# Expert layer of a decoder step: two of three prompt tiles by dense streamed tables instead of gathered rows

## The chip, the cores and the metric

One core of one Trainium2 chip runs the whole kernel. The metric is the device time of one launch in microseconds, median of several runs. The core has TensorE (PE; its weight loads are shown as PEld), VectorE (DVE), ScalarE (ACT), GpSimd (POOL) and SyncE (SP), and 16 DMA engines that move data between device memory and SBUF for all of them. SP and ACT start plain transfers; POOL starts the gathers that take row numbers from SBUF.

## The reference

One layer of a decoder on 512 prompt tokens and 32 sample tokens (8 sequences of 4), model width 1024, all in f32. A mixing part (projection, chunked gMLP, dilated window attention, output projection) comes first and is not touched. Then the expert layer (PEER), with 128 x 128 = 16384 experts, each a row of 1024 in `u_tab` and one in `v_tab`:

```python
q = (xb @ w_q).reshape(T, 8, 2, 128)
s = einsum('thcd,hcnd->thcn', q, sub_keys)      # 128 scores for each half key
s1, i1 = top_k(s[:, :, 0], 16); s2, i2 = top_k(s[:, :, 1], 16)
cand = s1[..., :, None] + s2[..., None, :]      # 16 x 16 pairs
top_s, pos = top_k(cand, 16); eid = (i1 * 128 + i2) at pos
g = softmax(top_s)
hid = gelu(einsum('thkd,td->thk', u_tab[eid], xb))
y = einsum('thk,thkd->td', g * hid, v_tab[eid]) # 8 heads x 16 = 128 experts a token
```

The layer's result is added to x, and a last RMSNorm gives y.

## The kernel before

Tokens lie in five tiles: tiles 0 to 3 of 128 prompt tokens and tile 4 (`SAMP`) with the 32 samples. `uv_tab` holds the u and the v row of an expert side by side, 8 KB. A slot is one of the 128 (head, rank) places of a token: one gather by POOL fetches for a slot one row for each of the 128 tokens of a tile. For the samples four groups of 32 partitions take four slots at a time, so 32 gathers do.

Tile 0 runs ahead, beside projection and attention of the others: 128 gathers of u rows (4 KB each, `gather_u`) are dotted with x on VectorE (`dots_to`, L1694). After attention 128 gathers of v rows (`gather_v`), now one token's 128 experts per gather, are weighed on TensorE (`weigh`, L896, four tokens at once in four column groups) into `acc`. These weighings are spread over the instruction stream of TensorE by `weigh_first(n)`: in `project_out` (output projection of tiles 1 to 4, L798), after `turn_xn` and in `half_queries` (L851). `JOBS` are the query projections, one for each head over tiles 1 to 4 (416 tokens); three of the eight run before the gathers of tile 1 start, the other five are put between the slots of tile 1 (`job_part`). `key_scores` (L871) multiplies by the sub keys.

Then for tiles 1, 2, 3 and the samples, 416 slots in one long loop, with a ring of `XR` = 6 buffers of 8 KB per partition:

- POOL: `gather_both` fetches u and v rows of a slot when the buffer is free.
- VectorE: `dot` (L1703) multiplies the u rows with x and sums, one hidden value per token. Between the dots run the 12 `LINKS` of each head's `route` (two rounds of top 8 of each half, candidates, top 16, one-hot pick of the numbers, L1547 to L1609), each link a step that waits for the one before.
- ScalarE: `weigh_slot` takes gelu of the hidden value (L1253), times the gate, and writes a diagonal matrix of the weights (`diag`, L1003).
- TensorE: `add_slot` (L907) multiplies diagonal and v rows, 2 x 512 columns, and sums in PSUM (`acc`).
- 20 slots of tile 1 (`BY_DVE`) are added by VectorE instead (`add_rows`, L1711).

After each tile ScalarE reads the sum (`read_sum`), squares it, and VectorE scales it (`finish_y`, L1724); SP stores y. Each engine runs its instructions in the order in which they are written; semaphores tie them.

## Time and profile before

| | |
|---|---|
| median of 3 runs | 1687.11 us (1685.46 to 1694.51) |
| profiled execution, span | 1709.3 us |
| TensorE matmul busy | 1404.9 us, 82% |
| VectorE busy | 1085.5 us, 64% |
| ScalarE busy | 634.5 us, 37% |
| moved by DMA | 664.8 MB, mean 389 GB/s |
| mean granted TensorE clock | 0.956 of full |

No separate time is given for the profiled execution; its span is what there is, and it is longer than the median of the other runs by 1.3%. Busy time says how long an engine had something to do, not that it set the pace: a matmul that waits in the pipeline counts too. The stages are: to about 430 us projection and attention with tile 0's u rows beside them; to 636 us output projection, queries and tile 0's v rows; to 1701 us the slots of tiles 1 to 4; then the last tile's norm and store.

### The profile page before, as it was taken

What the parts mean: (1) busy time and instruction counts of PE and PEld (TensorE: products, weight loads), DVE (VectorE), ACT (ScalarE), POOL (GpSimd) and SP (SyncE); (2) the same over time, 40 slices, a digit from 0 to 9 for tenths busy, and PEclk for the clock granted to TensorE, in tenths of its full rate; (3) what the DMA queues carried; (4) which work ended last, traced back from release to release, by engine and by line L of the source; (5) the groups of instructions that cost most, each with busy time, mean ns of one, the idle gap of its engine ahead of it and who ended that gap; (6) DMA issues with size and microseconds to landing.
All of it is one profiled execution on the core that took longest, in us unless ns stands there. A gap on an engine that the chain in (4) does not pass through costs nothing.

```text
span 1709.3 us, 17753 instructions
## 1 busy us (share of the span) xinstructions
PE 1404.9 (82%) x5164; PEld 622.7 (36%) x5164; DVE 1085.5 (64%) x2884; ACT 634.5 (37%) x1889; POOL 652.7 (38%) x703
## 2 busy tenths in 40 slices
PE   8999996768997978888878887777777777777786
PEld 5585663435333434334423232222223222222211
DVE  2459978868000046777766766666668888888654
ACT  2421113445211024344444454444445444444443
POOL 3034333322565653333333333333333333333332
PEclk9999996888998989999999999999999999999999
DMA  9798889999999999999999999999999999999997
GB/s 344 292 357 313 318 318 364 398 411 385 358 362 338 386 375 399 413 409 417 410 423 421 406 416 422 421 421 403 407 422 396 414 422 420 405 419 413 409 406 324
DMA packets 112144, 664.81 MB, mean 389 GB/s; under 512 B 13072, under 2 KB 14336, under 8 KB 52400
## 3 DMA queue, kind: packets, MB, share of 16 engines
q0 software_dynamic: 97824, 571.75, 83.4%
q1 hardware_dynamic: 14224, 91.93, 13.8%
q8 instruction: 42, 0.69, 0.2%
q14 instruction: 54, 0.44, 0.1%
HBM read 658.03 MB, written 5.60 MB: 388 GB/s over the span
## 4 chain that ended last, share of the span: by engine, by line
DMA 37%; PE 37%; issue 8%; ACT 7%; DVE 6%; another core or an unknown queue 3%; POOL 0%; ACTq 0%; SPq 0%; DVEq 0%; POOLq 0%
DMA area_r<-in_uv_tab,eid 36%; PE bank L907 11%; PE bank L627 9%; PE bank L851 4%; PE bank L896 4%; ACT area_c L1003 3%; PE bank L798 2%; DVE area_r L1703 2%; PE bank L558 1%; PE bank L871 1%; ACT L1253 1%; DVE area_x L1711 1%; DMA area_w<-in_w_in 1%; PE bank L767 1%
## 5 line engine op out<-in xcount | busy, mean ns | idle before, releaser
L907 PE MATMUL bank<-area_r,area_c 128*128 128x512 f32 (+1 forms) x1584 | 778.8, 624 | 213.8 <-ACT area_c L1003 212.8
L1873 POOL DMA_INDIRECT area_r<-in_uv_tab,eid x544 | 515.7, 948 | 944.0 <-PE bank L907 590.0
L1703 DVE CUSTOM_DVE_ANT_0 area_r<-area_r,bank 128x1024 f32<-128x1024 f32 x416 | 506.3, 1218 | 288.0 <-DMA area_r<-in_uv_tab,eid 287.3
L907 PEld LDWEIGHTS bank<-area_r,area_c 128*128 128x128 f32 (+1 forms) x1584 | 273.3, 188 | 713.0 <-issue 712.6
L1253 ACT ACTIVATE area_c<-hid 128x1 f32<-128x1 f32 x416 | 84.2, 202 | 538.8 <-DVE hid L1703 538.3
L1694 DVE CUSTOM_DVE_ANT_0 area_r<-area_r,bank 128x1024 f32<-128x1024 f32 x128 | 152.9, 1212 | 25.5 <-DMA area_r<-in_uv_tab,eid 22.7
L627 PE MATMUL bank<-area_w,area_t 128*128 128x384 f32 (+1 forms) x448 | 157.6, 509 | 4.1 <-DMA area_w<-in_w_in 3.5
L1003 ACT ACTIVATE area_c<-ident,area_c 128x128 f32<-128x128 f32 x364 | 146.1, 401 | 34.9 <-ACT area_c L1003 1.1
L1873 POOL DMA_INDIRECT area_r<-in_uv_tab,eidT x128 | 121.4, 948 | 82.0 <-issue 29.3
L1003 ACT ACTIVATE area_x<-bank 128x384 f32<-128x384 f32 (+8 forms) x123 | 49.9, 423 | 212.4 <-remote 59.4
L851 PE MATMUL bank<-area_t,area_w 128*128 128x416 f32 (+1 forms) x448 | 118.8, 418 | 6.1 <-issue 5.2
L1003 ACT ACTIVATE area_c<-gate,area_c 128x1 f32<-128x1 f32 x384 | 113.0, 294 | 13.9
L627 PEld LDWEIGHTS bank<-area_w,area_t 128*128 128x128 f32 x448 | 84.4, 192 | 68.0 <-issue 18.3
L851 PEld LDWEIGHTS bank<-area_t,area_w 128*128 128x128 f32 x448 | 70.4, 192 | 55.4 <-issue 54.1
L1397 DVE RECIPROCAL small<-small 128x1 f32<-128x1 f32 (+1 forms) x9 | 1.4, 158 | 113.3 <-issue 58.3
L896 PE MATMUL bank<-area_r,area_c 128*32 128x512 f32 x384 | 71.7, 633 | 0.9 <-issue 0.9
L1547 DVE MAX8 rt<-area_w 128x8 f32<-128x128 f32 (+1 forms) x80 | 19.3, 281 | 72.6 <-issue 52.0
L896 PE MATMUL bank<-area_r,area_v 128*32 128x512 f32 x128 | 64.4, 629 | 0.0
L798 PE MATMUL bank<-area_w,area_t 128*128 128x512 f32 x96 | 46.5, 631 | 1.7 <-issue 0.9
L1003 ACT ACTIVATE area_t<-bank 64x8 f32<-64x8 f32 (+5 forms) x111 | 28.6, 265 | 51.5 <-PE bank L558 28.3
L1487 DVE CUSTOM_DVE_ANT_0 area_x<-bank,area_c 128x256 f32<-128x256 f32 (+4 forms) x52 | 26.0, 535 | 23.9 <-PE bank L665 11.5
L1088 ACT ACTIVATE area_x<-area_x,att 128x256 f32<-128x256 f32 (+3 forms) x44 | 28.7, 653 | 31.2 <-DVE att L1487 19.1
(200 smaller groups left out, 1202.6 us busy)
## 6 DMA issues: line engine op xcount, KB each, us to landing
area_w<-in_w_in SPq DMA_DIRECT2D x12, 1536.0 KB, 11.1
area_w<-in_k_cache SPq DMA_DIRECT2D x8, 1920.0 KB
area_w<-in_w_q SPq DMA_DIRECT2D x14, 1024.0 KB, 6.8
area_r<-in_uv_tab,eid POOLq DMA_INDIRECT x544
area_w<-in_w_out SPq DMA_DIRECT2D x4, 2048.0 KB, 11.6
area_w<-in_v_cache SPq DMA_DIRECT2D x4, 1920.0 KB
area_v<-in_v_cache SPq DMA_DIRECT2D x4, 1152.0 KB
area_x<-in_x_p SPq DMA_DIRECT2D x6, 512.0 KB
```

Of the source, the lines that this page charges most:

```text
L627: mm = pe.matmul(out_half(u)[0:n, 0:w], featT[:, k, a:a + n], w_now[:, k, 0:w], start=(k == 0), stop=(k == KD - 1))
L798: mm = pe.matmul(ps[0:n, :], featT[:, k, a:a + n], w(k, c * 512, (c + 1) * 512), start=(k == 0), stop=False)
L851: mm = pe.matmul(half(4 + c)[:, 0:n], w[:, k, c * P:(c + 1) * P], featT[:, k, a:a + n], start=(k == 0), stop=(k == KD - 1))
L896: mm = pe.matmul(acc[CG * g:CG * g + CG, e, :], wd[g][:, c * CG:c * CG + CG], v_ring[s][:, e * 512:(e + 1) * 512], start=False, stop=False ...
L907: mm = pe.matmul(acc[0:n, c, :], diag[by_pe(i) % DG][:, 0:n], x_ring[s][:, D + c * 512:D + (c + 1) * 512], start=(i == 0), stop=False, ski ...
L1003: return nc.scalar.activation(out, src, ACT.Copy, scale=scale)
L1088: nc.scalar.activation(score_of(u)[0:r, 0:n], score_of(u)[0:r, 0:n], ACT.Exp, bias=st[0:r, 0:1], scale=-1.0, accum_out=st[0:r, 2:3]).then_ ...
L1253: nc.scalar.activation(bent[:, j:j + 1], hid[t % 2][:, j:j + 1], ACT.Gelu).then_inc(bent_ready, 1)
L1487: return vec.tensor_tensor_reduce(out=out, in0=scores, in1=counts, scale=-1.0, scalar=3e38, op0=ALU.add, op1=ALU.min, accum_out=least)
L1694: vec.tensor_tensor_reduce(out=u_ring[s], in0=u_ring[s], in1=x_cur, scale=1.0, scalar=0.0, op0=ALU.mult, op1=ALU.add, accum_out=hid[0][:, ...
L1703: vec.tensor_tensor_reduce(out=u, in0=u, in1=x_cur, scale=1.0, scalar=0.0, op0=ALU.mult, op1=ALU.add, accum_out=hid[t % 2][:, j:j + 1]).th ...
L1873: nc.gpsimd.indirect_dma_start(out=ring[s], out_offset=None, in_=table, in_offset=bass.IndirectOffsetOnAxis(ap=where, axis=0)).then_inc(la ...
```

## The change

Tiles 2 and 3 (`DENSE`, 256 tokens) no longer gather. Both tables are streamed once through SBUF in 128 blocks of 128 experts.

- **u pass.** `hidden(b)`: TensorE multiplies block b of u (stored transposed as a new input `u_blocks`, one load of 128 x 4 KB) with the 256 tokens, 8 matmuls of 256 columns; ScalarE takes gelu into `h_out`, and each four blocks go to device memory (`h_scratch`, 512 KB).
- **Gate matrix.** For every dense token a 128 x 128 matrix of gates is made, with the gates of its 128 slots at the place (first number, second number): `make_hots` on VectorE writes one-hot matrices for four tokens (one 512-wide and four 128-wide operations), `build_weights` multiplies them on TensorE (four matmuls of 128 columns), ScalarE copies (`read_built`). 64 such builds lie in u blocks 45 to 120; each eighth sends 2 MB to `w_scratch`.
- **v pass.** `weigh_block(b)`: VectorE multiplies the block's hidden values and gates, both loaded back (the gates 1 MB for eight blocks, in pieces of 1 KB), and `add_block(b)` on TensorE multiplies the result with block b of v, four matmuls of 512 columns.
- **Tile 1 and samples** are gathered as before, 160 pairs, ring of 5; but VectorE weighs and adds the v rows (`slot_add`), two slots behind the dot, and no diagonal is made. 72 slots of tile 1 lie at given blocks of the u pass, 56 in the v pass, and the 32 of the samples from v block 90 on.
- All eight query jobs come before the u pass, tile 0's last 20 v rows lie in its blocks 1 to 9, and `project_out` holds fewer of them. The ring of v rows is 8 deep instead of 12. Routing of tiles 2 and 3 lies in the u pass, that of the samples in the v pass.

The core of the diff:

```diff
-UR, VR, XR = 6, 12, 6
+UR, VR, XR = 6, 8, 5
+DENSE = range(2, NT - 1)
+NBUF, NA = 4, 4
+HQ, HLOADS = 4, 3
+TB, WQN = 32, 8
+BUILT = 4
-JOBS_AHEAD = 3
+ROWS_AT = range(1, 10, 2)
+BUILD_AT = [45 + w * 6 // 5 for w in range(NBUILD)]
+LINKS_FROM = {2: 4, 3: 42}
+LINKS_TO = {2: 40, 3: BUILD_AT[PER_TILE] - 4}
+SLOTS_U = [12 + i * 30 // 22 for i in range(22)] + [46 + 6 * i for i in range(6)] + [82 + i for i in range(44)]
+SLOTS_V = [1 + i * 3 // 2 for i in range(SLOTS - len(SLOTS_U))]
+SLOTS_S = [90 + i for i in range(SAMPLE_SLOTS)]
...
 # SP
+            for b in range(NBUF):
+                load_u(b)
             for i in range(HEADS + 3, len(JOBS)):
                 sp.wait_ge(q_done[1], i - 2)
                 load_wq(wq_ring[(i - HEADS) % 3], JOBS[i][0], wq_again[(i - HEADS) % 3])
...
+            for b in range(NBUF):
+                sp.wait_ge(h_done, NBLK + b - NBUF + 1)
+                load_v(b)
+                if b == 1:
+                    sp.wait_ge(built, NBUILD)
+                    sp.wait_ge(w_stored, 16 * (ND // TB))
+                    load_weights(0)
+                    load_weights(1)
+            for b in range(NBUF, NBLK):
+                sp.wait_ge(v_used, b - NBUF + 1)
+                load_v(b)
+                n = (b - 1) // HQ + 2
+                if b % HQ == 1 and n < NBLK // HQ:
+                    sp.wait_ge(a_ready, HQ * (n - HLOADS + 1))
+                    load_hidden(n)
+                m = (b - 1) // WQN + 1
+                if b % WQN == 1 and 2 <= m < NBLK // WQN:
+                    sp.wait_ge(a_ready, WQN * (m - 1))
+                    load_weights(m)
...
 # TensorE
+            def hidden(b):
+                pe.wait_ge(blk_in[b % NBUF], 16 * (b // NBUF + 1))
+                if b >= len(H_HALF):
+                    pe.wait_ge(gelued, b - len(H_HALF) + 1)
+                for k in range(KD):
+                    mm = pe.matmul(h_psum(b), blk[b % NBUF][:, k * P:(k + 1) * P], featT[:, k, DENSE[0] * P:DENSE[0] * P + ND],
+                                   start=(k == 0), stop=(k == KD - 1))
+                mm.then_inc(h_done, 1)
...
+            def build_weights(w):
+                pe.wait_ge(hots_ready, w + 1)
+                out = build_half(build_at["weights", w])
+                for q in range(BUILT):
+                    mm = pe.matmul(out[:, q * P:(q + 1) * P], hot_second[w % 2][:, q, :], hot_first[w % 2][:, q, :],
+                                   start=True, stop=True)
+                mm.then_inc(built, 1)
+
+            def add_block(b):
+                pe.wait_ge(blk_in[b % NBUF], 16 * ((NBLK + b) // NBUF + 1))
+                pe.wait_ge(a_ready, b + 1)
+                for t in DENSE:
+                    for c in range(2):
+                        mm = pe.matmul(sums[t][:, c, :], a_blk[b % NA][:, dense_no(t) * P:(dense_no(t) + 1) * P],
+                                       blk[b % NBUF][:, c * 512:(c + 1) * 512],
+                                       start=False, stop=(b == NBLK - 1), skip_group_check=True)
...
 # ScalarE
+            def gelu_block(b):
...
+                nc.scalar.activation(h_out[n % 2][:, b % HQ, :], h_psum(b), ACT.Gelu).then_inc(gelued, 1)
...
+            def read_built(w):
+                if w % PER_BATCH == 0 and w > 0:
+                    act.wait_ge(w_stored, 16 * (w // PER_BATCH))
+                act.wait_ge(built, w + 1)
...
 # VectorE
+            def slot(j):
+                first, last = (0, SLOTS - 1) if j < SLOTS else (SLOTS, SLOTS + SAMPLE_SLOTS - 1)
+                slot_dot(j)
+                if j >= first + 2:
+                    slot_add(j - 2)
...
+            def weigh_block(b):
+                if b % WQN == 0:
+                    dve.wait_ge(w_load_sem[b // WQN % 2], 16 * (b // WQN // 2 + 1))
+                if b % HQ == 0:
+                    dve.wait_ge(h_in_sem[b // HQ % HLOADS], 16 * (b // HQ // HLOADS + 1))
+                if b >= NA:
+                    dve.wait_ge(v_used, b - NA + 1)
+                out, hid_in = [x.rearrange("p (t k) -> p t k", k=TB) for x in (a_blk[b % NA], h_in[b // HQ % HLOADS][:, b % HQ, :])]
+                vec.tensor_tensor(out, w_load[b // WQN % 2][:, :, b % WQN, :], hid_in, ALU.mult).then_inc(a_ready, 1)
...
 # POOL
+            def gather_both(j):
+                if j == 0:
+                    pool.wait_ge(v_free, VR + V_FIRST)
...
+                if j >= XR:
+                    pool.wait_ge(x_added, j - XR + 1)
+                c = SLOTS + j if j < SLOTS else j - SLOTS
+                gather(x_ring, j % XR, uv_tab, eid[:, c:c + 1], x_landed)
```

## Rows read from the trace of the kernel before

**Rows 1.** The page: 40 slices of TensorE, its clock, DMA share, bandwidth.

```profile
PE   8999996768997978888878887777777777777786
PEclk9999996888998989999999999999999999999999
DMA  9798889999999999999999999999999999999997
GB/s 344 292 357 313 318 318 364 398 411 385 358 362 338 386 375 399 413 409 417 410 423 421 406 416 422 421 421 403 407 422 396 414 422 420 405 419 413 409 406 324
```

**Rows 2.** The page: the chain that ended last, by line.

```profile
DMA area_r<-in_uv_tab,eid 36%; PE bank L907 11%; PE bank L627 9%; PE bank L851 4%; PE bank L896 4%; ACT area_c L1003 3%; PE bank L798 2%; DVE area_r L1703 2%; PE bank L558 1%; PE bank L871 1%; ACT L1253 1%; DVE area_x L1711 1%; DMA area_w<-in_w_in 1%; PE bank L767 1%
```

**Rows 3.** Windows: stretch, length, busy PE, PEld, DVE, ACT, POOL, PEclk, DMA share, GB/s.

```profile
432.00:636.00 204.00, 183.34 (x909) 75.13 (x909) 25.51 (x83) 31.80 (x68) 121.82 (x130) 0.93 0.97 363
636.00:1701.00 1065.00, 848.72 (x1836) 315.42 (x1836) 759.03 (x1908) 459.06 (x1375) 389.29 (x412) 0.97 1.00 412
700.00:1600.00 900.00, 715.40 (x1540) 271.98 (x1539) 659.39 (x1713) 391.31 (x1166) 333.08 (x352) 0.98 1.01 414
```

**Rows 4.** Waits, 700 to 1600 us: us in total, times, longest.

```profile
POOL area_r L1873 <- PE bank L907: 505.5, 314, 5.8
ACT area_c L1253 <- DVE hid L1703: 451.5, 298, 3.6
DVE area_r L1703 <- DMA area_r<-in_uv_tab,eid: 222.1, 261, 2.5
PE bank L907 <- ACT area_c L1003: 180.7, 247, 3.0
```

**Rows 5.** Windows of 5 and 20 us, columns as in rows 3.

```profile
15.00:20.00 5.00, 5.00 (x15) 2.53 (x14) 0.00 (x0) 0.84 (x2) 5.00 (x10) 1.00 1.04 301
460.00:480.00 20.00, 20.00 (x90) 6.98 (x92) 0.12 (x1) 1.61 (x3) 13.12 (x14) 1.00 0.94 335
600.00:620.00 20.00, 20.00 (x104) 8.29 (x102) 5.86 (x21) 0.00 (x0) 13.77 (x15) 1.00 1.02 402
```

**Rows 6.** Matmuls: chain in time, timeline (start, length), one group by form.

```profile
147.01 15.68 PE bank L627 x48
...
461.07 0.62 PE L896 MATMUL bank<-area_r,area_c 128*32 128x512 f32 x3
...
461.50 0.62 PE L896 MATMUL bank<-area_r,area_c 128*32 128x512 f32 x3
...
573.47 3.06 PE L851 MATMUL bank<-area_t,area_w 128*128 128x416 f32 x8
...
L851 PE MATMUL bank<-area_t,area_w 128*128 128x128 f32 x192 | 23.0, 276 | 0.9 <-DVE area_t L1403 0.9
```

**Rows 7.** VectorE: groups by form (busy, mean ns), and one head's first and last step.

```profile
L1703 DVE CUSTOM_DVE_ANT_0 area_r<-area_r,bank 128x1024 f32<-128x1024 f32 x416 | 506.3, 1218 | 288.0 <-DMA area_r<-in_uv_tab,eid 287.3 <-DVE eid L1628 0.2
L1711 DVE SCALAR_TENSOR_TENSOR area_x<-area_r,area_c,area_x 128x1024 f32<-128x1024 f32 x20 | 25.6, 1281 | 0.0
L1600 DVE TENSOR_TENSOR area_w<-area_w,rt 128x512 f32<-128x512 f32 x32 | 22.1, 691 | 1.2
L1562 DVE TENSOR_TENSOR area_w<-rt 128x256 f32<-128x256 f32 x32 | 13.5, 420 | 0.9
L1506 DVE TENSOR_SCALAR area_r<-area_r,att 128x128 f32<-128x128 f32 x12 | 3.4, 287 | 0.4
...
596.95 0.49 DVE L1547 MAX8 rt<-area_w 128x8 f32<-128x128 f32 x2 [51.99 <-issue]
...
607.64 0.17 DVE L1609 SCALAR_TENSOR_TENSOR eid<-rt 128x16 uint32<-128x16 f32 x1 [0.15 <-DVE rt L1604]
```

**Rows 8.** Timeline of TensorE: end of the projections, key scores, first slots.

```profile
545.96 0.68 PE L558 MATMUL bank<-ident,area_v 32*128 32x32 f32 x8
...
595.69 2.45 PE L871 MATMUL bank<-area_r,area_x 128*128 128x128 f32 x16
...
639.70 5.96 PE L907 MATMUL bank<-area_r,area_c 128*128 128x512 f32 x7 [4.96 <-ACT area_c L1003]
```

**Rows 9.** Timeline of the last microseconds.

```profile
1704.00 1.01 ACT L1282 ACTIVATE area_v<-bank 32x1024 f32<-32x1024 f32 x1 [0.54 <-PE bank L907]
...
1707.02 0.33 SPq L548 DMA_DIRECT2D out_y_s<-area_x  x1
```

**Rows 10.** Chain in time: a gather from issue to landing.

```profile
880.31 10.26 DMA area_r<-in_uv_tab,eid
```

More of the change, by code:

```diff
@@ L385, in build @@
         score_at = {th: i for i, th in enumerate(SCORED)}
-        def job_part(j):
-            i, p = HEADS + JOBS_AHEAD + j // TOPK, {3: 0, 8: 1, 13: 2}.get(j % TOPK)
-            return (i, p) if p is not None and i < len(JOBS) else None
         def job_tokens(i):
@@ L833, in turn_xn, with half_queries @@
                     mm.then_inc(xn_turned, 1)
[L836 to L840 removed]
+            def half_queries(i, c):
                 h = JOBS[i][0]
@@ new lines, in build_half, with turn_picked @@
+            def build_half(r):
+                if r >= len(BUILD_HALF):
+                    pe.wait_ge(build_read, r - len(BUILD_HALF) + 1)
+                return half(BUILD_HALF[r % len(BUILD_HALF)])
+            def turn_picked(t):
+                pe.wait_ge(tile_gated, dense_no(t) + 1)
+                out = build_half(build_at["picked", t])
+                for i, src in enumerate((picked[t % 2][:, 0, :], picked[t % 2][:, 1, :], gate[:])):
+                    mm = turn(out[:, i * P:(i + 1) * P], src, P)
+                mm.then_inc(idx_turned, 1)
@@ new lines, in _ @@
+            left = HEADS * LINKS
+            for b in range(NBLK):
+                weigh_block(b)
+                if b < LINKS_S_TO:
+                    n = -(-left // (LINKS_S_TO - b))
+                    left -= n
+                    go_on(links[SAMP], n)
+                if b == LINKS_S_TO:
+                    go_on(links[SAMP])
+                    set_x_samp()
+                    sample_indices()
+                if b == GATES_S:
+                    finish_gates(SAMP)
+                if b == 8:
+                    finish_y(0)
+                if b == Y_ONE_AT:
+                    finish_y(1)
+                for j, at in enumerate(SLOTS_V):
+                    if b == at:
+                        slot(len(SLOTS_U) + j)
+                for j, at in enumerate(SLOTS_S):
+                    if b == at:
+                        slot(SLOTS + j)
@@ L1849, in _ @@
+            for i in range(2, NT):
+                finish_y(i)
         @block.gpsimd
```

584 lines of the change are left out of this document (331 added, 253 removed).

## The prediction, made before the changed kernel ran

> **What bounds the kernel now.** I read the page first: the 40 slices show the DMA engines at nine tenths or more from the eighth slice on, TensorE at seven tenths in the second half, and bandwidth at 400 to 420 GB/s there [rows 1]. The chain of work says the same: 36% of the span is a gather of expert rows [rows 2]. Third, the windows. From 636 to 1701 us the 416 gathers of tiles 1, 2, 3 and the samples run, the DMA share is 1.00, and TensorE is busy 849 of 1065 us [rows 3]. The waits tell who follows whom there: VectorE waits for gathers, ScalarE for VectorE, TensorE for ScalarE, POOL for TensorE to free a ring slot [rows 4]. The reader should see one saturated resource (16 DMA engines moving 8 KB rows) and everything else paced by it. Between 432 and 636 us (output projection, queries, v rows of tile 0) it is nearer a draw: TensorE 183 of 204 us, DMA share 0.97 [rows 3].
>
> So two prices decide: a byte by DMA and a column by TensorE.
>
> **Prices.** A pair gather (u and v row, 128 x 8 KB, 1.05 MB) costs 2.53 us at 414 GB/s [rows 3]. A load of 128 rows of 4 KB (0.52 MB): in 600 to 620 us, where nearly only such rows moved, 402 GB/s, so 1.31 us; at 460 to 480 us 335 GB/s at share 0.94, so 1.47 us [rows 5]. I take 1.33, because the new ones are dense and not gathered, and keep 1.26 (the rate of the 8 KB rows) to 1.47 as bounds. Seen by one engine, an 8 KB piece takes 2.53 x 16 / 128 = 316 ns and a 4 KB piece 166 to 184 ns, so a 1 KB piece by the same line costs 54 to 85 ns; 1024 of them (one 1 MB load of gate weights) 3.4 to 5.4 us, I take 4.1. Bound from above: the only full-share window well below 350 GB/s had 301 [rows 5].
> The Trainium skill (DMA: Bandwidth & Descriptors, section iDMA fabric) gives 408.7 GB/s for a stream of 1 MiB DMAs with 4 KiB rows, which would be 1.28 us for a dense block; no row here shows a dense stream alone, and the sum would end about 8 us earlier by it.
>
> TensorE at the full clock of 2.4 GHz: an f32 matmul is two passes; 512 columns take 0.43 us a pass, 384 take 15.68 / 48 = 0.327, 416 0.351 (the eight of 3.06 us less the last one's modelled tail), 128 take 23.0 / 192 = 0.120 [rows 6]. 256 columns lie on that line at 0.213 to 0.225; I take 0.22. VectorE: dot 1.22 + 0.08, scaled add 1.28, so 2.65 a slot with a gap; one head of routing 10.9 us for 12 links, 0.91 each; a 512-wide tensor op 0.69, a 128-wide scalar op 0.29 [rows 7].
>
> **Stage A, 432 us to the first dense block.** The projection part ended at 546 us [rows 8]. It loses 28 of its 72 v rows (four go at once in 1.72 us, so 0.43 each): 12 us, end 534. Then all eight query jobs of tiles 1 to 3 and samples come before the dense pass; before, three did, and five lay in tile 1's gathers. One job: 2 x 16 passes of 0.351 + 16 passes of key scores in 2.45 us [rows 8] + 8 v rows at 0.43 + 0.5 of switching = 17.7; eight are 142, so 676, and 678 with the copy of the last scores. DMA needs 64 x 1.33 + 8 MB of query weights (20 us) = 105, so it hides. VectorE's routing of tile 1 (10.9 a head against 17.7 a job) hides too. On SP the first four u blocks are issued ahead of the remaining query weights: 2 MB, hidden by ring depth.
> Before, the first pair was used at 635.8, so this stage costs 42 us in which DMA is a third idle.
>
> **The u pass (128 blocks).** TensorE 16 x 0.22 = 3.5 us a block. By stretches, each the larger of the two resources:
> - blocks 0 to 12: 42 + the last 20 v rows 9 = 51 (TensorE).
> - 12 to 42, 22 slots: TensorE 105; DMA 30 x (1.33 + 0.33 for the hidden store) + 22 x 2.53 = 106; VectorE 22 x 2.65 + about 60 links x 0.91 = 113, less the lead it has by then. I take 110.
> - 42 to 82, with 33 builds of gate weights (8 passes of 128 columns and a switch, 1.0 us each): 140 + 33 = 173. DMA only about 100. VectorE: 33 builds of 0.69 + 4 x 0.29 + 0.15 = 2.0, 96 links, 6 slots: 169, just under.
> - 82 to 126, one slot a block: DMA 1.33 + 0.33 + 0.52 (2 MB store of gate weights each 9.6 blocks) + 2.53 = 4.71, 44 of them 207; TensorE 185.
> - the last two: 7.
> Sum 548, end at 1226.
>
> **Between the passes** SP loads v blocks 0 and 1, then waits for the last weight store, then two loads of 1 MB that VectorE's first product needs: about 10 us until TensorE runs, part of it at half clock (after such a pause seven passes took 5.96 us [rows 8], twice 0.43 each). Bounds 4 and 15.
>
> **The v pass.** TensorE 8 x 0.43 = 3.45 a block, VectorE's product 0.42 (256 wide, like the routing's sums).
> - 0 to 84, 56 slots: DMA 1.33 + 0.33 + 4.1 / 8 + 2.53 / 1.5 = 3.86, so 324 (TensorE 290).
> - 84 to 122, 32 sample slots: DMA 38 x 2.17 + 32 x 2.53 = 163 (TensorE 131).
> - 122 to 128 and the samples' sum: 24 (TensorE).
> Sum 511, end at 1747; the tail (square, root, scale, store) 9 us, somewhat more than the 5 from the last square on now [rows 9]. **Span 1756.** I add 9 us for coupling: SP now waits on `a_ready` every fourth block ahead of the next v loads, whose lead falls from four blocks to two or three; ScalarE waits inside the block loop for a 2 MB store every eighth build, with gelu of the next blocks queued behind it and TensorE behind three banks; a pair gather is released by VectorE's add, three in flight. None alone reaches the pace: a gather takes 10.26 us to land now [rows 10], over three in flight 3.4 us a slot, below 4.7. If that cover is gone (landing over 14 us) the slots add 1 us each, 76 of them.
> **Total 1765** against 1709.3.
>
> Why does less traffic not help? Removed: 256 pair gathers, 648 us of DMA. Added: dense u and v 256 x 1.33 = 340, hidden out and in 84, gate weights out 42 and in 65: 531. Net 117 us. But TensorE goes from 849 us of work with slack to 973 without (448 + 442 + 64 + 9 + 10), and the remaining 160 pairs are bunched where both are full.
>
> **Profile against timed runs.** The span is 1709.3 and the median 1687.1, so the factor is 0.987: 1765 becomes 1742 us, 3.3% slower. What a measurement of this kernel can tell from no change is about 0.5%.
>
> **Rivals.**
> 1. *TensorE paces all of it (faster).* Place: the stretches where I let DMA exceed it, by 22, 5, 34 and 32 us, plus 5 of the pause and 9 of coupling, 107 in all. If all goes, the span is 1658, 1637 timed. For it: dense rows may move at 420 GB/s or more, as slices now do [rows 1]. Against: blocks 82 to 126 alone need a pair gather in 2.0 us, and none here is under 2.5. It turns the sign once 64 of the 107 us are gone; at the 1.26 price only about 20 go. Faster: 0.15.
> 2. *VectorE becomes the bound in the u pass.* Blocks 4 to 82 hold 184 links, 28 slots and 33 builds: 307 us against TensorE's 315. For it: a draw, with in-order waits for landings. Against: it may run ahead until block 40. If builds or links cost 15% more or a landing stalls it, 30 to 45 us more: 1775 to 1785. 0.15.
> 3. *The gate weights come back slowly.* They are read in pieces of 1 KB, 16 KB apart, eight tiles 2 MB apart. At half of the 360 GB/s of 4 KB rows a load costs 5.8, at a quarter 11.6: 0.2 to 0.9 us a block over 122 blocks, 25 to 115 us, so 1767 to 1855. No row shows such a pattern. 0.12.
> The Trainium skill (DMA: Bandwidth & Descriptors, section Latency and other measured facts) speaks for this rival: with rows a large power of two apart it measured half of the full rate at the worst, which it ascribes to memory channels; no run here shows it yet.
> 4. *It comes out even*, between 1679 and 1695, by some of rival 1: 0.10.
> Forecast (two resources in turn, 1700 to 1775): 0.48.
> That the change does not do what it says would show as a stall per slot; it is in rival 2.
>
> **Numbers.** 1742 us. The range: below, part of rival 1; above, rival 2 and the milder half of rival 3: 1668 to 1805. Faster by over 0.5% 0.15, within 0.5% 0.10, slower by over 0.5% 0.75.
>
> **What would show it.** Hidden matmuls at 0.22 us a pass and 3.5 us a block in blocks 0 to 12; the first dense block at 678 us; DMA share near 1.0 in blocks 82 to 126 and the v pass, near 0.6 in blocks 42 to 82; about 4.7 and 3.9 us a block there; waits of TensorE for VectorE's products in the v pass and behind them VectorE waiting for gathers. If dense blocks move above 430 GB/s, or TensorE is busy 97% in both passes, rival 1 holds. If VectorE has no idle time in blocks 42 to 82 while TensorE waits, rival 2. If a 1 MB weight load takes over 10 us, rival 3.

## The result, and the profile after

The changed kernel takes 1795.56 us (median of 4 runs, 1779.58 to 1801.02) against 1686.28 us (1684.92 to 1694.51) for the kernel before, measured side by side: ratio 1.063, interval 1.058 to 1.068. It is slower, as forecast, by nearly twice as much (6.3% where 3.3% stood). The profiled execution has a span of 1792.7 us and a mean granted clock of 0.945. In all runs here the time of an execution is its span plus 1.7 to 2.1 us.

The page of the kernel after, first line and the slices that answer to [rows 1]:

```profile
PE 1604.2 (89%) x7170; PEld 1000.6 (56%) x7170; DVE 1094.6 (61%) x2902; ACT 364.4 (20%) x1087; POOL 433.5 (24%) x447
...
PE   8999987788999999999999778877999999877768
...
PEclk9999997779999999999999989988999999988889
DMA  9789999999788878998776899989999999988983
GB/s 349 302 333 331 314 351 391 385 376 401 253 325 308 304 247 328 385 409 304 254 249 225 290 358 352 355 317 385 361 396 391 384 407 387 346 330 346 359 339 117
```

Before, one row of digits stood at nine and the other had slack. Now both stand at nine, but in turn, and there are two dips: slices 23 to 28 (986 to 1255 us) and 35 to 39 (1524 to 1748 us). There TensorE is at six to eight tenths, DMA at eight to nine, and the bandwidth at 290 to 385 GB/s, so neither resource is full. The chain that ended last can be followed back only to 1122 us here, 37% of the span, so it tells of the end of the u pass and of the v pass and can't be set against [rows 2] share by share. In that part a matmul line and the load of v blocks lead.

```profile
PE bank L1009 18%; DMA area_r<-in_uv_tab 11%; PE bank L980 2%; DMA area_r<-w_scratch 1%; DMA w_scratch<-area_w 1%; DMA area_r<-in_u_blocks 1%; PE bank L1000 1%; DVE area_x L1858 0%; DVE area_r L1883 0%; DVE area_r L1880 0%; ACT area_w L1129 0%; ACT area_v L1373 0%; PE bank L1023 0%; PE bank L962 0%; ACT area_v L1129 0%
```

The windows of the kernel after, by stretch (columns as in [rows 3]: length, busy time of the five engines, clock, DMA share, GB/s). They are, within a block or two, u blocks 0 to 42, 42 to 82, 82 to 126; v blocks 0 to 84, 84 to 122; the rest:

```profile
662.00:822.00 160.00, 158.59 (x760) 130.65 (x759) 118.80 (x357) 32.64 (x96) 38.17 (x40) 1.00 0.96 370
822.00:984.00 162.00, 162.00 (x868) 145.60 (x867) 125.75 (x427) 34.95 (x86) 5.83 (x6) 1.00 0.71 246
984.00:1241.00 257.00, 207.42 (x1025) 178.70 (x1024) 159.47 (x297) 54.20 (x170) 52.39 (x44) 0.93 0.91 340
1251.00:1567.00 316.00, 294.19 (x656) 127.53 (x657) 219.99 (x507) 29.16 (x113) 61.29 (x53) 0.97 0.98 382
1567.00:1754.00 187.00, 140.29 (x304) 60.75 (x303) 101.25 (x166) 22.02 (x74) 30.85 (x32) 0.87 0.88 336
1754.00:1793.00 39.00, 32.55 (x75) 12.98 (x73) 6.78 (x12) 4.21 (x9) 0.00 (x0) 0.97 0.31 105
```

The first two rows are TensorE at its limit (158.6 of 160, 162.0 of 162). The fourth is DMA at its limit (0.98) with TensorE close behind. The third and fifth are neither: TensorE is idle for 50 and 47 us in them. The granted clock is lower there too (0.93 and 0.87), and the matmuls right behind a pause take about twice their time (in the timeline below eight of 128 columns 2.08 us, 1.16 at 1135.89 in the same kernel); what this adds was not measured by itself.

Against the forecast, with block b dated by ScalarE's gelu in the u pass and by VectorE's product in the v pass (the last three columns are kernels of the experiments; the row between the passes runs from u block 127, and 4 us from block 126 to 127, 7 forecast for the last two blocks, are left out):

| stretch, us | forecast | after | two stages | split loads | no slots |
|---|---|---|---|---|---|
| first block at | 678 | 665.4 | 664.5 | 662.6 | 656.8 |
| u 0 to 12 | 51 | 51.8 | 51.9 | 51.9 | 51.8 |
| u 12 to 42 | 110 | 107.6 | 107.6 | 108.0 | 105.3 |
| u 42 to 82 | 173 | 166.8 | 166.5 | 167.6 | 166.5 |
| u 82 to 126 | 207 | **245.6** | **208.8** | 250.4 | 181.4 |
| between the passes | 10 | 9.8 | 15.4 | 10.0 | 1.6 |
| v 0 to 84 | 324 | 315.7 | 326.9 | 311.0 | 279.0 |
| v 84 to 122 | 163 | **187.2** | 187.5 | **165.5** | 130.4 |
| v 122 to the end | 33 | 38.8 | 38.7 | 38.8 | 39.0 |

Two stretches carry the surplus: 39 and 24 us. The other rows, with the last blocks and the end, are 26 us shorter than forecast together, so that the span is 37 us above the 1756 of the sum before coupling.

**The first dip, u blocks 82 to 126.** The waits of the kernel after there (engine, line, what it waited for: us in total, times, longest):

```profile
POOL area_r L2075 <- DVE area_x L1858: 172.4, 35, 17.8
...
DVE area_x L1858 <- ACT area_v L1129: 79.4, 24, 14.9
...
PE bank L1000 <- DVE area_r L1883: 44.7, 15, 11.5
ACT area_w L1129 <- DMA w_scratch<-area_w: 38.1, 4, 12.2
```

Read from the bottom it is one story. ScalarE waits four times for a store of 2 MB to `w_scratch`, because there is one staging buffer (`read_built`); VectorE waits for ScalarE's weight column of a slot; TensorE waits for VectorE's one-hot matrices; POOL waits for VectorE's add. The timeline of one such stall (start, length, engine, line, operation, in brackets the idle time before it and its releaser):

```profile
996.86 0.33 ACTq L1394 DMA_DIRECT2D w_scratch<-area_w  x1
...
1000.99 3.62 PE L980 MATMUL bank<-area_t,area_r 128*128 128x256 f32 x16
1009.05 0.60 ACT L1129 ACTIVATE area_w<-bank 128x512 f32<-128x512 f32 x1 [8.31 <-DMA w_scratch<-area_w]
...
1010.24 1.28 DVE L1858 SCALAR_TENSOR_TENSOR area_x<-area_r,area_v,area_x 128x1024 f32<-128x1024 f32 x1 [14.88 <-ACT area_v L1129]
...
1011.80 1.14 POOL L2075 DMA_INDIRECT area_r<-in_uv_tab,eid  x1 [17.79 <-DVE area_x L1858]
...
1013.21 2.08 PE L1000 MATMUL bank<-area_r 128*128 128x128 f32 x8 [8.60 <-DVE area_r L1883]
```

The store is issued at 996.86. The next copy into the same buffer starts at 1009.05, 12.2 us later. VectorE has stood 14.9 us, POOL has issued no gather for 17.8 us, TensorE stands 8.6 us. After it both resources have a backlog, and as my sum has both nearly full in this stretch, I take it that they can't work it off.

**The second dip, v blocks 84 to 122.** The waits of the kernel after there:

```profile
DVE area_w L1895 <- PE bank L1009: 71.2, 25, 14.6
...
PE bank L1009 <- DMA area_r<-in_uv_tab: 46.7, 5, 13.8
```

TensorE waits five times for a v block, 46.7 us, and VectorE's product then waits for TensorE to free a buffer. SyncE's queue (first four lines) and TensorE (last two) around one of them:

```profile
1622.13 0.33 SPq L578 DMA_DIRECT2D area_r<-in_uv_tab  x1
1622.56 0.39 SPq L586 DMA_DIRECT2D area_w<-h_scratch  x1
1623.00 0.58 SPq L582 DMA_DIRECT2D area_w<-w_scratch  x1
1625.57 10.63 SPq L578 DMA_DIRECT2D area_r<-in_uv_tab  x4
```
```profile
1619.79 16.04 PE L1009 MATMUL bank<-area_r,area_w 128*128 128x512 f32 x37
1646.04 14.35 PE L1009 MATMUL bank<-area_r,area_w 128*128 128x512 f32 x27 [10.21 <-DMA area_r<-in_uv_tab]
```

Every eighth block a load of 1 MB of gate weights (L582) goes out on SyncE's queue ahead of the next v block, while the samples' gathers run beside. The block behind it, issued at 1625.57, is used at 1646.04, after a pause of 10.2 us. The timelines of both engines, block by block, show the pattern in this stretch: a block is mostly used 10.1 us after its issue (three blocks of 3.4 us), but the four behind each 1 MB load 20.5 to 26.1 us after it. The longest pause is 13.8 us.

### The profile page after: what moved, and what is told of

The parts are those of the page before. It is cut to its first block and busy times, and to the rows that moved or that the text cites. A ratio compares the mean times of both kernels' runs of the same rounds, so it can differ in the third digit from the quotient of the medians.

```text
span 1792.7 us, 20728 instructions
## 1 busy us (share of the span) xinstructions
PE 1604.2 (89%) x7170; PEld 1000.6 (56%) x7170; DVE 1094.6 (61%) x2902; ACT 364.4 (20%) x1087; POOL 433.5 (24%) x447
## 5 line engine op out<-in xcount | busy, mean ns | idle before, releaser
L1009 PE MATMUL bank<-area_r,area_w 128*128 128x512 f32 x1024 | 463.4, 615 | 76.6 <-DMA area_r<-in_uv_tab 67.9
L2075 POOL DMA_INDIRECT area_r<-in_uv_tab,eid x256 | 262.7, 1026 | 976.3 <-DVE area_x L1858 552.9
L980 PE MATMUL bank<-area_t,area_r 128*128 128x256 f32 x2048 | 462.4, 383 | 6.6 <-DMA area_r<-in_u_blocks 5.8
L980 PEld LDWEIGHTS bank<-area_t,area_r 128*128 128x128 f32 x2048 | 387.8, 193 | 64.8 <-DMA area_r<-in_u_blocks 8.9
L1009 PEld LDWEIGHTS bank<-area_r,area_w 128*128 128x128 f32 x1024 | 200.6, 197 | 339.5 <-issue 256.8
L1858 DVE SCALAR_TENSOR_TENSOR area_x<-area_r,area_v,area_x 128x1024 f32<-128x1024 f32 x102 | 130.2, 1276 | 83.1 <-ACT area_v L1129 82.7
L1838 DVE CUSTOM_DVE_ANT_0 area_r<-area_r,bank 128x1024 f32<-128x1024 f32 x128 | 153.1, 1212 | 39.2 <-DMA area_r<-in_uv_tab,eid 39.0
L1846 DVE CUSTOM_DVE_ANT_0 area_r<-area_r,area_v 128x1024 f32<-128x1024 f32 x102 | 123.5, 1211 | 19.4 <-DMA area_r<-in_uv_tab,eid 19.4
L714 PEld LDWEIGHTS bank<-area_w,area_t 128*128 128x128 f32 x448 | 84.4, 192 | 67.9 <-issue 18.7
L1000 PE MATMUL bank<-area_r 128*128 128x128 f32 x512 | 73.1, 288 | 45.0 <-DVE area_r L1883 44.7
L1000 PEld LDWEIGHTS bank<-area_r 128*128 128x128 f32 x512 | 68.7, 200 | 55.0 <-DVE area_r L1883 52.6
## 6 DMA issues: line engine op xcount, KB each, us to landing
area_w<-in_w_in SPq DMA_DIRECT2D x12, 1536.0 KB, 10.5
area_w<-in_k_cache SPq DMA_DIRECT2D x8, 1920.0 KB, 14.4
```

What stands on the lines that cost most here:

```text
L714: mm = pe.matmul(out_half(u)[0:n, 0:w], featT[:, k, a:a + n], w_now[:, k, 0:w], start=(k == 0), stop=(k == KD - 1))
L980: mm = pe.matmul(h_psum(b), blk[b % NBUF][:, k * P:(k + 1) * P], featT[:, k, DENSE[0] * P:DENSE[0] * P + ND], start=(k == 0), stop=(k == K ...
L1000: mm = pe.matmul(out[:, q * P:(q + 1) * P], hot_second[w % 2][:, q, :], hot_first[w % 2][:, q, :], start=True, stop=True)
L1009: mm = pe.matmul(sums[t][:, c, :], a_blk[b % NA][:, dense_no(t) * P:(dense_no(t) + 1) * P], blk[b % NBUF][:, c * 512:(c + 1) * 512], start ...
L1838: vec.tensor_tensor_reduce(out=u_ring[s], in0=u_ring[s], in1=x_cur, scale=1.0, scalar=0.0, op0=ALU.mult, op1=ALU.add, accum_out=hid[0][:, ...
L1846: vec.tensor_tensor_reduce(out=u, in0=u, in1=xn_tile[GATHERED] if j < SLOTS else x_samp, scale=1.0, scalar=0.0, op0=ALU.mult, op1=ALU.add, ...
```

## Experiments

The first theory, formed from these views: two bursts of the gate matrix's round trip, the store and the load, each hit an engine or a queue that works in order, and the two waits are the surplus over my sums. Rivals: the pattern of the load (1 KB pieces) is slow in itself; or the pairs that are left cost more than I priced.

### A second staging buffer for the store

```diff
...
             def read_built(w):
-                if w % PER_BATCH == 0 and w > 0:
-                    act.wait_ge(w_stored, 16 * (w // PER_BATCH))
+                m = w // PER_BATCH
+                if w % PER_BATCH == 0 and m >= 2:
+                    act.wait_ge(w_stored[m % 2], (64 if m % 2 else 16) * (m // 2))
```

Odd batches go into `w_parts`, four free pieces of SBUF, by four copies a build and four stores a batch.

> Changed kernel with a second staging buffer for the gate matrix (four free pieces of 4 KB per partition), so that ScalarE no longer waits for a 2 MB store before it copies the next build. Theory A (the bursts cost time because of the waits they cause): the five stalls of 8 to 20 us between u blocks 45 and 122 go, 35 to 50 us off, ratio to before 1.035 to 1.045. Rival B (the DMA engines are simply full there): ScalarE's wait goes, but TensorE then waits for blocks or VectorE for gathers instead; under 12 us off, ratio above 1.055.

Measured: 1768.72 us, ratio 1.048 (1.045 to 1.051), 27 us off, less than the 35 to 50 expected. Blocks 82 to 126 fell from 245.6 to 208.8 us; 207 was my sum. Window and waits of this kernel there:

```profile
984.00:1199.00 215.00, 195.78 (x1004) 169.51 (x1002) 153.85 (x288) 56.16 (x223) 49.62 (x42) 0.98 0.99 385
```
```profile
DVE area_x L1870 <- ACT area_v L1131: 42.7, 22, 7.4
...
PE bank L1002 <- DVE area_r L1895: 19.0, 16, 3.3
```

ScalarE's wait for the store is gone from the list, VectorE's longest wait for a weight column has halved (14.9 to 7.4), and DMA is full (0.99, was 0.91). The stretch is then bound as the sum had it. The cure gained 37 us there and gave 17 back: the pause between the passes grew by 6, and v blocks 0 to 84 took 11 more.

### The gate weights' load cut in eight

```diff
+            def load_weight_part(m, t):
+                src = w_scratch[t, :, m * WQN * TB:(m + 1) * WQN * TB]
...
-                if b % WQN == 1 and 2 <= m < NBLK // WQN:
-                    sp.wait_ge(a_ready, WQN * (m - 1))
-                    load_weights(m)
+                if 1 <= b % WQN <= 4 and 2 <= m < NBLK // WQN:
+                    if b % WQN == 1:
+                        sp.wait_ge(a_ready, WQN * (m - 1))
+                    for t in range(2 * (b % WQN) - 2, 2 * (b % WQN)):
+                        load_weight_part(m, t)
```

The same bytes in the same pieces of 1 KB, but as eight loads of 128 KB, two behind each of four v blocks.

> Changed kernel, with each 1 MB load of gate weights cut into eight loads of 128 KB (same 1 KB pieces, same bytes), two behind each of four v blocks instead of all at once. Theory A (a burst in SP's queue delays the v blocks behind it): the pause that VectorE and TensorE make every eighth v block (5 to 8 us early, 16 us beside the sample slots) shrinks by half or more, 40 us off, ratio about 1.04. Rival B (bytes): no more than 10 us off. Rival C (small pieces are slow): nothing off either.

Measured: 1766.47 us, ratio 1.046 (1.042 to 1.050), 29 us off where 40 were expected. Blocks 84 to 122 fell from 187.2 to 165.5 us; my sum was 163. Window and wait of this kernel:

```profile
1565.00:1730.00 165.00, 140.12 (x303) 59.45 (x302) 100.99 (x165) 22.01 (x74) 30.78 (x32) 0.94 0.98 382
```
```profile
PE bank L1016 <- DMA area_r<-in_uv_tab: 24.9, 9, 6.1
```

TensorE's waits for v blocks halve (46.7 to 24.9 us), and the DMA share goes from 0.88 to 0.98 at 382 GB/s. Bytes and pieces are the same, so 22 of the 24 us of the dip go with the order and the size of the loads on the queue.

### The gate weights read in 8 KB pieces

```diff
-                src = w_scratch[:, :, m * WQN * TB:(m + 1) * WQN * TB].rearrange("t p f -> p t f")
+                src = w_scratch[m % 8][:, m // 8 * 2 * D:(m // 8 + 1) * 2 * D]
```

As many bytes, read from other places of `w_scratch`; the work is otherwise the same.

> Changed kernel that reads as many bytes of gate weights, but 128 pieces of 8 KB instead of 1024 of 1 KB for each load. The rows read are other rows, so tiles 2 and 3 get other gates. Rival C (1 KB pieces, 16 KB apart, are slow): 1024 pieces cost 10 us and more of the engines, so 60 us or more off, ratio 1.025 or below. My price of 4.1 us against about 2.5: 14 x 1.6 = 22 us off at the most. Theory A: the burst is shorter, but still ahead of the blocks, 15 to 25 us off, ratio about 1.05.

Measured: 1768.75 us, ratio 1.049 (1.046 to 1.052), 27 us off. The two forms of this load (issue to landing) in this kernel, and below them in the kernel after:

```profile
area_r<-w_scratch SPq DMA_DIRECT2D x8, 1024.0 KB, 12.8
area_w<-w_scratch SPq DMA_DIRECT2D x8, 1024.0 KB, 13.2
```
```profile
area_r<-w_scratch SPq DMA_DIRECT2D x8, 1024.0 KB, 15.7
area_w<-w_scratch SPq DMA_DIRECT2D x8, 1024.0 KB, 14.4
```

A load lands 1.2 or 2.9 us sooner, 8 x 1.2 + 8 x 2.9 = 33 us for all. Of the 27 us measured, 22 lie in the v pass's two stretches (6 and 16); 4 lie ahead of the first block, which the edit doesn't touch. TensorE's waits for v blocks in the second stretch fell from 46.7 to 30.0 us. My third rival wanted 25 to 115 us on top of a sum that charges 4.1 us a load already. Its mildest end is thus there in size, but the split loads, with the small pieces kept, give as much. My reading is that a v block's time behind the burst is what costs, and that the small pieces make the burst somewhat longer. The sign that I had named for this rival, over 10 us for a load, is met (14.4 and 15.7 us), but it was a poor sign: loads in 8 KB pieces take 13.2 and 12.8 us on the same busy queue. By the Trainium skill (DMA: Bandwidth & Descriptors, section Latency and other measured facts) rows 4 and 8 MiB apart ran at about half of the full rate in copies from device memory to device memory. This case doesn't test that rule: in both forms the rows of the partitions are 16 KB apart, and only the small pieces come from eight tiles 2 MB apart.

### No pairs at all

```diff
-                for j, at in enumerate(SLOTS_U):
-                    if b == at:
-                        slot(j)
...
-            for j in range(SLOTS + SAMPLE_SLOTS):
-                gather_both(j)
```

Left out: the gathers, dots, weights and adds of tile 1 and of the samples, so that their feed-forward part is missing. What remains is what the dense tiles cost.

> Changed kernel without gathers, dots and adds of tile 1 and samples in both passes; both lack their experts' part. What is left is the dense work. If TensorE sets its pace: 3.45 us a block plus 0.9 us a build in the u pass, 3.45 in the v pass, so u pass 500 us, v pass 445 us, span about 1625 (ratio 0.96). If the dense streams themselves (4 KB rows, 1 KB pieces, stores) were slow, pauses remain and the span stays above 1680.

Measured: 1617.07 us, ratio 0.959 (0.956 to 0.961). Its windows of u blocks 82 to 126 and of most of the v pass:

```profile
980.00:1162.00 182.00, 182.00 (x972) 163.75 (x971) 53.29 (x155) 34.68 (x79) 0.00 (x0) 1.00 0.67 226
1167.00:1594.00 427.00, 426.60 (x994) 188.97 (x995) 116.22 (x411) 6.23 (x12) 0.00 (x0) 1.00 0.69 229
```

TensorE has no idle time and DMA is a third idle. 44 blocks took 181.4 us where I had 185 and the v pass goes at 3.3 to 3.45 us a block. The stores and loads of the gate matrix cost nothing here. So the bursts hurt only together with the gathers. In the same stretch ScalarE still waits four times for the store, but for 17.3 us in all and 6.0 at most (38.1 and 12.2 in the kernel after), and no weight column is queued behind it that VectorE waits for. The run doesn't separate these two. Between this kernel and the one after lie 179 us for 160 pairs, 1.1 us a pair, less than half of 2.53: the rest of their transfer did hide.

### Both cures together

The two edits above in one kernel.

> Changed kernel with both cures, the second staging buffer and the cut gate loads. Each alone took 25 to 28 us. If they act on two separate stretches (u blocks 82 to 126 by the store, v blocks 84 to 122 by the load), both come: 50 us off, about 1745 us, ratio 1.034; stretches 208 and 165 us as my sum had them. If what one frees is given back in the other (the engines' queues just move the jam), 30 us, ratio 1.045.

Measured: 1728.65 us (1726.19 to 1730.40), ratio 1.024 (1.022 to 1.027), 67 us off, more than the two cures alone give (27 and 29) and more than the 50 expected. Blocks 82 to 126 took 208.9, v 0 to 84 309.3, v 84 to 122 165.0 us. My reading is that each cure alone moves load into the other's bad place (the 11 us in v 0 to 84 under the first); together nothing is given back there. Only the pause between the passes stays longer, 15.4 us.

### The remaining pairs spread over the blocks that had room

All three variants keep the cures and change at which block a pair (in the third also a build) stands. For the earlier samples their routing also ends at v block 68 instead of 84. The first takes ten pairs from the v pass into u blocks 60 to 80 and starts the samples at v block 74:

```diff
-SLOTS_U = [12 + i * 30 // 22 for i in range(22)] + [46 + 6 * i for i in range(6)] + [82 + i for i in range(44)]
-SLOTS_S = [90 + i for i in range(SAMPLE_SLOTS)]
+SLOTS_U = [12 + i * 30 // 22 for i in range(22)] + [46, 53] + [60 + i * 3 // 2 for i in range(14)] + [82 + i for i in range(44)]
+SLOTS_S = [74 + i * 3 // 2 for i in range(SAMPLE_SLOTS)]
```

> Both cures, and ten slots of tile 1 moved from the v pass into u blocks 60 to 80, the sample slots begun at v block 74 and spread at one each 1.5 blocks. By my prices the u stretch has VectorE and DMA to spare after block 60 and stays at 168 us, and the v pass (462 us by DMA, 421 by TensorE, to block 122) loses 14 us: ratio 1.025. If VectorE is already the limit in blocks 42 to 82, the u stretch grows by 10 slots x 2.65 = 26 us and the ratio rises to 1.04.

Measured: 1713.19 us (1708.28 to 1719.64), ratio 1.017 (1.014 to 1.020), the best version of the dense scheme that I found, better than the 1.025 expected. Its windows of the v pass (to block 84, and the 166 us behind it, of which the last 24 lie behind block 122):

```profile
1215.00:1524.00 309.00, 286.65 (x650) 123.76 (x651) 222.17 (x528) 32.39 (x115) 59.40 (x53) 0.98 0.99 384
1524.00:1690.00 166.00, 157.95 (x361) 68.13 (x360) 79.26 (x120) 13.93 (x52) 20.61 (x23) 0.99 0.91 352
```

In the same second window with the cures alone TensorE was busy 142.5 us at share 0.98; now 158.0 at 0.91. The lower share comes from those last 24 us (0.41); from 1524 to 1666 us, the 142.1 us of v blocks 84 to 122, it is 0.99. So the v pass is still bound by DMA and became shorter because it holds ten pairs less: 447.8 instead of 474.3 us to block 122, and 10 x 2.53 = 25. In u blocks 42 to 82 the ten cost nothing (167.8 us, 166.5 with the cures alone).

The second lays them evenly, three pairs to four blocks from u block 60 on and in the v pass, five samples to seven blocks from v block 78:

```diff
-SLOTS_U = [12 + i * 30 // 22 for i in range(22)] + [46 + 6 * i for i in range(6)] + [82 + i for i in range(44)]
-SLOTS_V = [1 + i * 3 // 2 for i in range(SLOTS - len(SLOTS_U))]
-SLOTS_S = [90 + i for i in range(SAMPLE_SLOTS)]
+SLOTS_U = [12 + i * 30 // 22 for i in range(22)] + [46, 53] + [60 + i * 4 // 3 for i in range(50)]
+SLOTS_V = [1 + i * 4 // 3 for i in range(SLOTS - len(SLOTS_U))]
+SLOTS_S = [78 + i * 7 // 5 for i in range(SAMPLE_SLOTS)]
```

> Both cures, and the pairs spread as evenly as VectorE lets them: one slot each 4/3 blocks from u block 60 to 125 (33 instead of 44 in blocks 82 to 126), 54 in v blocks 1 to 71, sample slots from v block 78 at one each 1.4. Same bytes as before. Theory A (in each stretch the larger of DMA's and TensorE's sum): u blocks 82 to 126 fall from 210 to 187 us, the v pass takes the bytes over and grows by 20, ratio 1.012 to 1.016. If what costs is jams and not sums, an even load goes below the sums: ratio 1.00 to 1.008.

Measured: 1728.69 us, ratio 1.023 (1.020 to 1.027): no gain over the cures, a miss. Blocks 42 to 82 grew by 15 us, to 182.0, where I had only seen room on DMA. Window of u blocks 42 to 82 and two waits in it:

```profile
820.00:987.00 167.00, 157.85 (x816) 139.80 (x815) 145.19 (x451) 38.25 (x132) 15.65 (x16) 0.97 0.81 288
```
```profile
DVE area_x L1877 <- ACT area_v L1138: 9.8, 4, 4.4
PE bank L1009 <- DVE area_r L1902: 9.1, 5, 3.7
```

The same window of the kernel with moved pairs, which has 16 pairs in these blocks where this one has 19:

```profile
820.00:987.00 167.00, 166.74 (x894) 149.56 (x894) 152.53 (x458) 43.37 (x150) 16.34 (x17) 1.00 0.84 305
```

VectorE does more there (152.5 us), and TensorE has next to no gap. So VectorE's work alone is not the bound here, and my second rival is not shown in that form. What differs is a wait: VectorE stands 9.8 us for ScalarE's weight columns, with the one-hots behind it, and then TensorE stands 9.1 us for these. The moved kernel has no wait of VectorE for a column in this window. ScalarE makes the column of a pair two blocks behind the pair's dot, and VectorE uses it at the block of the next pair but one. With one pair each 3/2 blocks that is always three blocks later; with one each 4/3 it is two for every third pair, and the first wait, 4.4 us, is at the first of these pairs. That this lead is the cause fits both traces, but no run varied it alone.

The v pass grew too, by its own prices: 84 x 2.17 + 59 x 2.53 = 332 us, measured 328.6.

The third has the even pairs and also makes the last builds earlier, to shorten the pause before the v pass:

```diff
-BUILD_AT = [45 + w * 6 // 5 for w in range(NBUILD)]
+BUILD_AT = [45 + w * 9 // 8 for w in range(NBUILD)]
```

> The same, with the 64 builds one each 9/8 block instead of 6/5, so the last at u block 115 and its 2 MB store at 116 instead of 121. The pause of 12 to 15 us between the passes (last store, then the first two gate loads) is a chain of landings, so 6 to 10 us go, ratio 1.008. If VectorE is at its limit between blocks 42 and 82, that stretch grows by 6 us and nothing is won.

Measured: 1736.80 us, ratio 1.032 (1.027 to 1.037). That is a miss as well, 1.008 was expected. The pause fell from 9.8 to 4.2 us, and u blocks 42 to 126 grew from 377.8 to 389.5: 2 us in blocks 42 to 82 and 9 in 82 to 126, where TensorE's waits for u blocks rose from 2.9 to 10.5 us. Why stays open.

### The price of a dense block by DMA alone

```diff
-                for k in range(KD):
+                for k in range(2):
...
-                    for c in range(2):
+                    for c in range(1):
```

No pairs as above, and further left out: six of eight matmuls of a u block, two of four of a v block. So tiles 2 and 3 are incomplete too, and TensorE has less to do than DMA.

> To measure what a dense block costs the DMA engines: no slots as in the kernel without them, and TensorE does two of eight matmuls a block in the u pass and two of four in the v pass (the rest of the sums is left out). TensorE then needs 0.9 and 1.7 us a block. My prices: u blocks 10 to 38 at 1.66 us each (1.33 and 0.33), v blocks at 2.17. At the rate of 8 KB rows 1.57 and 2.0; at 1.47 for 4 KB rows 1.84 and 2.5. If the 1 KB pieces are slow the v blocks come at 2.6 or above while the u blocks keep 1.66.

Measured: 1346.87 us. Windows in the u pass (stores of hidden values beside) and in the v pass (all loads):

```profile
715.00:765.00 50.00, 33.10 (x101) 22.20 (x100) 28.08 (x113) 11.71 (x27) 0.00 (x0) 0.83 0.90 315
1020.00:1320.00 300.00, 238.00 (x476) 96.64 (x475) 110.71 (x392) 3.13 (x6) 0.00 (x0) 0.91 0.87 310
```

The blocks came at 2.1 and 2.4 us, with DMA not quite full. An estimate for full share is 315 / 0.90 = 350 GB/s and 310 / 0.87 = 356 GB/s. A u block with its store (0.655 MB) is then 1.87 us, I had 1.66; a v block with hidden values and gates (0.786 MB) 2.2 us, I had 2.17. The v pass, with its 1 KB pieces, is not slower a byte than the u pass without them, which speaks against the third rival once more. The slices of the kernel before at 420 GB/s, on which rival 1 leaned, were gathers of 8 KB rows; dense rows of 4 KB, with stores or small loads among them, don't reach that here. The Trainium skill (DMA: Bandwidth & Descriptors, section iDMA fabric) has 408.7 GB/s for a single stream of loads with 4 KiB rows. This run, with stores and other loads among them, shows less.

### The kernel before with all query jobs first

```diff
-JOBS_AHEAD = 3
+JOBS_AHEAD = 8
...
-                queries(i, 4)
+                queries(i, 4 if i < HEADS + 3 else 0)
```

With `JOBS_AHEAD` at 8 the 20 adds that VectorE did for tile 1 go back to TensorE.

> The kernel BEFORE with all eight query jobs ahead of tile 1's gathers, as the change has them, and nothing else new (the 20 adds of VectorE go back to TensorE). Five jobs of 14 us leave the gather loop, which DMA paces anyway, and stand in a stage where DMA only has v rows left. My account: the loop shortens by nothing, the first pair comes 50 to 70 us later, ratio 1.03 to 1.04. If the gathers hide it, 1.00 to 1.01.

Measured: 1748.43 us (1740.44 to 1752.99), ratio 1.035 (1.031 to 1.039), 61 us more than the kernel before. Its windows:

```profile
636.00:700.00 64.00, 55.84 (x209) 30.34 (x207) 10.58 (x29) 21.16 (x55) 8.50 (x10) 0.97 0.26 98
700.00:1740.00 1040.00, 799.59 (x1650) 276.15 (x1651) 726.35 (x1864) 446.05 (x1338) 379.91 (x405) 0.99 1.00 413
```

For 64 us TensorE computes queries and the DMA engines are three quarters idle; after it the loop of gathers takes 1057 us, 8 less than before (1065). So the five jobs cost at most 8 us where TensorE had slack, and ahead of it they make the kernel 61 us longer. From the first pair at 682.5 to the end of the span are 1066.6 us; in the dense kernel with both cures it is 1068.1 from the first block at 659.9. So the streamed passes, cured, are no faster than the gathers of the same tiles; what they carry besides is tile 0's last 20 v rows (9 us by my price). The stage ahead is what they cost.

### A second look at the kernel before

The kernel before, unchanged, one profile.

> The kernel before once more with a profile, to see whether its profiled execution is long by nature. In my sum I scaled by 1687.1 / 1709.3; the seven other kernels' profiled executions lie within 0.5% of their medians. If the first trace of before was a slow draw: span 1680 to 1692. If profiling lengthens this kernel (more gathers, more semaphore events): 1705 or more.

Measured: 1684.11 us with a span of 1682.3 us, 27 us shorter than the span of the first profile (1709.3). Windows to compare with [rows 3]:

```profile
432.00:636.00 204.00, 195.42 (x936) 80.87 (x935) 42.50 (x125) 40.78 (x99) 122.98 (x130) 0.98 1.01 393
636.00:1673.00 1037.00, 819.89 (x1789) 302.15 (x1788) 740.18 (x1862) 444.98 (x1336) 380.58 (x402) 0.99 1.00 414
```

The first pair was used at 610.6 us instead of 634.7, and the loop of gathers took 1062 us instead of 1065. The output projection began at 417.0 instead of 432.1. So of the 27 us 15 lie ahead of it, 9 between it and the first pair (194 us instead of 203, for the same 909 matmuls and 184 and 183 us of busy TensorE, at a granted clock of 0.98 instead of 0.93), and 3 in the loop. The first window above shows more work (195 us) only because it reaches 25 us into the gathers. The first trace was a long draw, by its stages ahead of the gathers, and nothing proportional to the span.

## Why the prediction was right and where it failed

**Sign and mechanism: right.** Fewer bytes and no gain, since TensorE has 3.5 us of work a block and the pairs that remain meet it where DMA is full as well. The sign is explained by the experiments in two parts: of 109 us (timed), 67 go with the two cures, and what is left, 42 us, is less than the 61 us that the query jobs ahead cost the kernel before. Two things that I had named as signs did not come: the DMA share in blocks 82 to 126 was 0.91 and not near 1.0, and in the v pass TensorE waited for v blocks, not for VectorE's products (67.9 us in 14 waits against 8.7 us in one, 1251 to 1754 us).

**Prices of the engines: right.** 3.47 us a u block (I had 3.5), blocks 0 to 12 in 51.8 (51), builds and blocks 42 to 82 in 166.8 (173), the v pass without pairs at 3.3 to 3.45 us a block. The pause was 9.8 (10). The jobs took 17.4 us each (17.7); the timeline of the kernel after shows two in a row:

```profile
536.75 5.85 PE L931 MATMUL bank<-area_t,area_w 128*128 128x416 f32 x16
...
554.14 5.85 PE L931 MATMUL bank<-area_t,area_w 128*128 128x416 f32 x16
```

**First failing step: coupling at 9 us.** "None alone reaches the pace" was wrong for two of the three waits it names. I had priced the wait of ScalarE by who was directly behind it (gelu, three banks of cover) and overlooked the third queue member: the weight column of the next slot, for which VectorE waits in order, with the one-hots of the next build behind that. And I had compared landing times of gathers with the pace, but not the landing of a v block behind a 1 MB burst with its two or three blocks of lead: at 3.45 us a block that lead is 7 to 10 us (10.1 in the trace), and blocks behind a burst were used 20.5 us and more after their issue, with pauses up to 13.8. The term cost 39 + 24 = 63 us instead of 9; the two cures, each for one of the waits, bring the stretches to 208.8 and 165.5, within 3 us of the sums of 207 and 163.

**Second failing step: the factor 0.987.** It took a long draw of one trace for a property of all. The excess of the first trace sat in the stages before 636 us. The span of the kernel after is 1792.7 and its median 1795.6, factor 1.002, though its output projection too began late in this trace (429.3). That is 26 of the 54 us that I was short (1792.7 x 0.987 = 1769.4). The sum itself was short by 28: 1792.7 against 1765.

**Terms that were off and cancelled.** Without them the forecast would have been further off, and that it was not is luck. The first block came at 665 instead of 678: the projection part ended at 515.9 instead of 534, with the clock at 0.98 from 429 to 516 us where it was 0.92 before, from 432 to 546. A dense u block costs DMA 1.87 instead of 1.66 us by the estimate above, near the bound of 1.47 a load that I had kept and not the 1.33 that I took. This is hidden in most of the u pass, and shows as a share of 0.71 in blocks 42 to 82 where I had said near 0.6. In blocks 82 to 126 the sum with it would be 44 x 4.92 = 216 us, while the cured kernels took 209, so the match with 207 is partly luck or the estimate is high; no run separates the two. By the pages' queue shares DMA work fell by 78 us (97.5% of 1709.3 to 88.6% of 1792.7) and not by 117; 128 x 0.21 = 27 us of the difference are this price. The end, from v block 122 on, was 39 us instead of 33, which stays unexplained in detail.

**Rivals.** TensorE paces all: only without the pairs (ratio 0.959). VectorE bound: not in this layout; with 16 pairs in blocks 42 to 82 it was busy 152.5 of 167 us and cost nothing; with 19 the stretch grew by 15 us, with VectorE waiting for weight columns, which is nearer to the coupling than to the rival's work. Slow gate loads: the pattern adds 1 to 3 us of landing, and as much of the loss went away with the pieces kept small; its size was near the mild end, its cause for the most part the place on the queue. Even: not reached; the best version is 1.7% above the kernel before.

**Open.** A kernel that keeps five query jobs in the slack of another stage and streams the tables was not tried, since in the dense scheme routing of tiles 2 and 3 needs those jobs before block 42. Nor was a second staging buffer without the odd batches' four small copies, or a pair's add three slots behind its dot instead of two: with the second buffer VectorE still waits 42.7 us for weight columns in blocks 82 to 126.

## What to carry to other kernels

Before a transfer of 1 MB or more is put on a queue or behind a single buffer, list everything queued behind it on that engine and, for each, the engine that waits for it in order; my reading of the two dips, not measured as a rule, is that the chain's price is the landing time less the shortest lead on it, not less the nearest one. Replacing a bandwidth bound by fewer bytes and more matmul gains only while the other engine has slack, and work that lay in that slack for nothing (here five query jobs, 61 us) has to be paid for. Take the factor between a trace and the median from two traces, or find the stage in which the trace is long, before scaling with it.

## What the runs showed of the hardware that was not expected

- The first stages take different time from execution to execution: the first load of output-projection weights into TensorE was at 432.1 and at 417.0 us in two profiles of the kernel before, and at 429.3 us in the kernel after against 413.2 to 425.8 in its nine variants, whose work up to there is the same.
- A dense v block of 512 KB takes 9.0 us to land at the median. Beside gathers and right behind a 1 MB load TensorE could go on only 20.5 us after its issue (1625.57 to 1646.04), and once 25.6. The 2 MB stores take 13.0:

```profile
area_r<-in_uv_tab SPq DMA_DIRECT2D x128, 512.0 KB, 9.0
...
w_scratch<-area_w ACTq DMA_DIRECT2D x8, 2048.0 KB, 13.0
```

- Dense 4 KB rows with small loads or stores among them come to 350 to 356 GB/s at full share by the estimate from the thin kernel, gathers of 8 KB rows ran at 413 to 414.
